# Beta and decay in v's second weight tile, retention's PSUM banks from bank 4, and unread products ahead of eight transposes

## What is computed

```python
def even_mixer(x, rel_bias, w_in, conv_w, a_log, dt_bias, norm_w, w_out):
    q_a, k_a, v_a, z_a, b_a, a_a, q_b, k_b, v_b = jnp.split(x @ w_in, EVEN_SPLITS, axis=-1)
    ...
    beta = jax.nn.sigmoid(b_a.astype(f32))
    g = -jnp.exp(a_log.astype(f32)) * jax.nn.softplus(a_a.astype(f32) + dt_bias.astype(f32))
    o_a = gated_delta_rule(q_a, k_a, v_a, g, beta)
    ...
    o_b = dilated_attention(q_b.reshape(shp), k_b.reshape(shp), v_b.reshape(shp), rel_bias)

# in diff_attention, for each head and block of 128 queries
    p = jax.nn.softmax(s, axis=-1)
    attn = p[:, :, 0] - lam * p[:, :, 1]
    return jnp.einsum('bhqk,bhkv->bhqv', attn.astype(v.dtype), vt)
```

## Time and profile before

| | us |
|---|---|
| median of 3 runs | 1760.88 |
| lowest and highest | 1760.47, 1765.22 |
| span of the profiled execution | 1759.8 |
| TensorE busy in it | 1648.0 |
| VectorE busy | 937.4 |
| ScalarE busy | 627.9 |
| GpSimd busy | 228.9 |

### The profile page before, as it was taken

The page is one execution under the profiler, slowest core; times in us unless marked ns, Lnnn a source line. Parts: engine busy times, 40 slices in busy tenths (PEclk is TensorE's granted clock), DMA queues, the critical chain, the costliest instruction groups (busy, mean ns, idle before and its releaser), DMA issues. The chain is left out here.

```text
span 1759.8 us, 25741 instructions
## 1 busy us (share of the span) xinstructions
PE 1648.0 (94%) x10372; PEld 1226.0 (70%) x10372; DVE 937.4 (53%) x1668; ACT 627.9 (36%) x1050; POOL 228.9 (13%) x217
## 2 busy tenths in 40 slices
PE   9999998999999989999999989997789999899966
PEld 8788875699988544899888864442379898643422
DVE  1285664688642565788554766131166967732212
ACT  1035322466531224566446541110144456411101
POOL 0000000054202121263101302000000300020000
PEclk9999999999999999999999999998999999999989
DMA  8322186445553666455424766999954655699996
GB/s 328 144 96 96 66 337 268 170 166 216 192 215 122 238 275 251 162 197 193 168 96 144 301 249 260 421 421 421 390 217 144 201 225 177 259 408 421 421 420 265
DMA packets 50336, 429.45 MB, mean 244 GB/s; under 512 B 5788, under 2 KB 6048, under 8 KB 9248
## 3 DMA queue, kind: packets, MB, share of 16 engines
q1 hardware_dynamic: 47232, 417.59, 61.0%
q0 software_dynamic: 2256, 7.88, 1.3%
q10 hardware_dynamic: 720, 2.23, 0.3%
HBM read 426.62 MB, written 1.05 MB: 243 GB/s over the span
## 5 line engine op out<-in xcount | busy, mean ns | idle before, releaser
L88 ACT ACTIVATE arena<-ps 128x384 f32<-128x384 f32 (+5 forms) x221 | 96.4, 436 | 512.3 <-PE ps L82 305.5
L82 PE MATMUL ps<-ringx,arena 128*64 128x512 f32 (+1 forms) x1088 | 251.0, 623 | 29.6 <-DMA ring<-in_mu 19.7
L82 PE MATMUL ps<-xsplit_f,wsplit_f 128*128 128x256 f32 x2112 | 256.0, 284 | 4.2 <-ACT xsplit_f L88 2.6
L82 PEld LDWEIGHTS ps<-xsplit_f,wsplit_f 128*128 128x128 f32 x2112 | 254.1, 192 | 6.6 <-ACT xsplit_f L88 4.2
L82 PE MATMUL ps<-ring,arena 128*64 128x512 f32 (+2 forms) x768 | 238.7, 618 | 15.7 <-DMA ringx<-in_md 6.9
L91 DVE TENSOR_TENSOR wsplit_f<-ring,wsplit_f 128x1024 fp32r<-128x1024 f32 x132 | 180.2, 1369 | 70.3 <-ACT wsplit_f L88 70.3
L82 PEld LDWEIGHTS ps<-ringx,arena 128*64 128x64 f32 (+1 forms) x1088 | 75.3, 130 | 168.7 <-issue 157.7
L82 PE MATMUL ps<-xTs,ring 128*128 128x256 f32 (+1 forms) x960 | 186.0, 353 | 2.2 <-ACT xTs L88 2.2
L82 PEld LDWEIGHTS ps<-xTs,ring 128*128 128x128 f32 x960 | 161.4, 191 | 23.3 <-issue 4.8
L88 ACT ACTIVATE wsplit_f<-ring 128x1024 fp32r<-128x1024 f32 x132 | 138.1, 1051 | 57.4 <-PE ps L82 56.5
L91 DVE TENSOR_TENSOR ringlo<-ring,ringhi 128x1024 fp32r<-128x1024 f32 x88 | 120.4, 1384 | 58.6 <-ACT ringhi L88 58.3
(11 more groups left out here) (204 smaller groups left out, 2315.8 us busy)
## 6 DMA issues: line engine op xcount, KB each, us to landing
ring<-in_wu SPq DMA_DIRECT2D x22, 2048.0 KB, 8.5
ringx<-in_mg SPq DMA_DIRECT2D x44, 1024.0 KB, 15.5
ringx<-in_mu SPq DMA_DIRECT2D x44, 1024.0 KB, 17.9
ring<-in_ada SPq DMA_DIRECT2D x20, 2048.0 KB, 8.7
ringx<-in_md SPq DMA_DIRECT2D x32, 1024.0 KB, 17.3
ring<-in_md SPq DMA_DIRECT2D x32, 1024.0 KB, 23.7
ring<-in_wd SPq DMA_DIRECT2D x10, 2048.0 KB, 8.2
ring<-in_mg SPq DMA_DIRECT2D x20, 1024.0 KB, 15.6
```

Source lines behind the costliest of these rows:

```text
L82: return self.e.matmul(o, l, r, start=start, stop=stop, skip_group_check=True)
L88: return self.e.activation(o, i, f, **k)
```

## The change

Three edits.

First, the twelve columns of beta and decay are appended to the tile wev2, which becomes 268 columns wide, and wba is gone from the parameters. wev2 is loaded and multiplied before wev. ScalarE copies the twelve columns of each half out of vb1's bank ahead of its evacuation, VectorE has no copy of its own and works out beta and decay before it evacuates vb0. The bank ba is gone, so the count of R8 is one lower in everything that follows, up to retention.

Second, warm(2) stands ahead of the wait for each of the eight softmax results in the odd mixer: 16 unread products.

Third, retention sets R8's count to 4 after its own warm(4): the first rows' transposes take banks 4 and 5, the four products 6, 7, 0 and 1, the second rows' transposes 2 and 3.

```diff
 def all_loads():
-    out = [("we", 6), ("we", 7), ("we", 8), ("wev",), ("wev2",)] + [("we", j) for j in range(6)]
+    out = [("we", 6), ("we", 7), ("we", 8), ("wev2",), ("wev",)] + [("we", j) for j in range(6)]
...
-          ("lwg", 256), ("rw", 128), ("wba", 96), ("wgd", 128)]
+          ("lwg", 256), ("rw", 128), ("wgd", 128)]
...
-        return 2048 if name[0] in ("wev2", "wdl") else 4096
+        return {"wev2": 2144, "wdl": 2048}.get(name[0], 4096)
...
+            proj_rows(("wev2",), "vb1", 268)
             proj_rows(("wev",), "vb0", 512)
-            proj_rows(("wev2",), "vb1", 256)
-            b = bank("ba")
-            wba = C("wba").rearrange("p (k n) -> p k n", k=8)
-            for h in range(2):
-                for k in range(8):
-                    r = mm(b[:, 12 * h:12 * h + 12], xT[:, k, h * 128:h * 128 + 128], wba[:, k, :], k == 0, k == 7)
-            r.then_inc(s_pe, t.did("ba"))
             t.wait_ge(s_hank, 16)
...
                 elif k == 2:
+                    warm(2)
                     t.wait_ge(*v("df_p", u))
                     b = bank("dfT", u)
...
         def ret():
             warm(4, ring=MOE_BANKS)
+            ps.turn[R8] = 4
             first_tiles(6, ("wr", 0), "pr", Q.xT)
...
-            for h in range(2):
-                evac_rows("vb0", h, E.vbt[:, h, 0:512])
-            v.note("vbt")
-            v.wait_ge(*t("ba"))
-            copy(small[:, 0:24], ps("ba")[:, 0:24]).then_inc(s_dve, v.did("free", "ba"))
-            v.note("ba")
             ba = two(small[:, 0:24])
             v.wait_ge(*a("beta_exp"))
...
                 .then_inc(s_dve, v.did("decay"))
+            for h in range(2):
+                evac_rows("vb0", h, E.vbt[:, h, 0:512])
+            v.note("vbt")
             v.wait_ge(*t("gam"))
...
             for h in range(2):
+                a.wait_ge(*t("vb1", h))
+                copy(small[:, 12 * h:12 * h + 12], ps("vb1", h)[:, 256:268]).then_inc(s_act, a.did("ba"))
                 evac_rows("vb1", h, E.vbt[:, h, 512:768])
             a.note("vbt")
             ba = small[:, 0:24].rearrange("p (t n) -> p t n", t=2)
-            a.wait_ge(*v("ba"))
```

More of the change, by code:

```diff
@@ L3502 @@
     ins["wev"] = tiles(we[:, 4620:5132], 8, 512)
-    ins["wev2"] = tiles(we[:, 5132:5388], 8, 256)
+    ins["wev2"] = tiles(_np.concatenate([we[:, 5132:5388], we[:, 3072:3084]], 1), 8, 268)
     ins["woe"] = rowtiles(a["w_out_even"][0], 4)
@@ L3544 @@
         "lwg": pad(a["gla_w_gate"][0]), "rw": tiles(a["router_w_2"], 8, 16)[0],
-        "wba": tiles(we[:, 3072:3084], 8, 12)[0], "wgd": tiles(wo[:, 3072:3088], 8, 16)[0],
+        "wgd": tiles(wo[:, 3072:3088], 8, 16)[0],
     }
```

## The result

The changed kernel takes 1746.18 us (1744.34 to 1749.63, 4 runs) against 1762.35 for the kernel before on the same chip (4 runs). The forecast was 8.5 us faster, 1752.4, with 1747.5 as the low end of the range. The sign is right, the size is little more than half of what came, and the time lies outside the range.

What follows compares the result with a forecast made beforehand. TensorE's queue was taken as the bound nearly everywhere, with DMA full in two expert stages. The terms -3.9 + 0.2 - 1.4 - 3.4 = -8.5 us gave 1752.4 us, with an 8-in-10 range of 1747.5 to 1758.5.

Steps and rivals of the forecast that it cites:

- A, the products and the wait: At v's rows: narrow products gone, second rows 12 columns wider, -3.17 us; TensorE's wait for the decay chain gone, -0.59.
- the load term: At TensorE's first weight load, about 25 us: parameter block 48 KB shorter, -0.1 us.
- Sum of A: -3.9: Beta and decay riding with v's second rows: -3.17 - 0.59 - 0.1 us, on TensorE's own queue before the attention products.
- B: Unread products ahead of the third stage's eight transposes: +1.0 us cost, one of two clock places kept, -1.4 net.
- the clock of one place: Third stage, behind the waits near 610 and 658 us: 2.4 us lost at each; the first taken as kept.
- waits as short as those at 638: Third stage: products at 638.64 ran at full speed behind waits of 0.60 and 0.58 us, so such waits do no harm.
- C: Retention's start from bank 4: TensorE starts 1.9 us earlier, plus half of the clock's gain, -3.4 us.
- the 2.9 us of clock: Retention, 1291 to 1297 us, clock 0.50: between 0 and 2.9 us kept after the shorter wait; half taken.
- What the prediction quoted from the Trainium skill on transposes: At retention's start: transposes don't count as TensorE activity, so part C keeps no clock, -1.9 us, total 1753.9.
- The shift of banks: Eight-bank ring up to retention: later tiles move one bank, one becomes later around 938 us; +0.2 us, bounds 0 and +0.5.
- The loads keep their own time: Rival: expert stages' loads not tied to earlier stages, gains become waits there; 1757.5 us or no change, chance 0.11.
- The slower rival: Third stage: unread products delay the chain they wait beside, full 6.9 us stands; +1.3, 1762.2 us, chance 0.05.

Runs made afterwards that it cites:

- e1: The changed kernel without the unread products and without retention's bank count set to 4; ratio 0.9921 to the kernel before, -13.9 us.
- e7: e1 with the eight-bank ring's count raised by one behind v's rows, so each later tile keeps its old bank; ratio 0.9933 to the kernel before.
- e11: The changed kernel with 64 unused columns behind the parameters in SBUF; ratio 0.9900 to the kernel before.
- e14: The changed kernel with unread products only before the four transposes whose waits cover them, eight in place of sixteen; ratio 0.9906 to the kernel before.
- e2: The kernel before with only the two unread products added before each of the eight softmax waits; ratio 0.9994, -1.1 us.
- e4: The changed kernel measured again as it stands; ratio 0.9907 to the kernel before, -16.4 us.

## Why the prediction was right in direction and short by nearly half

**A, the products and the wait: right, with a small term short.** -4.1 against -3.76 without the load term. The chain is hidden and nothing took its place. The 0.1 for the shorter load can't be told: at 25 us the traces lie between 0.4 us earlier and 1.2 later than the kernel before, with part A or without. The 0.4 at VectorE's copy was not in the sum.

**A, the whole: wrong, and here the prediction fell.** The step that failed is "Sum of A: -3.9", as a list of what A does. The SBUF layout wasn't in it: I costed the shorter parameter block as 48 KB less to load, and never as 384 bytes by which 81920 bytes of weight buffers move in each partition. 4.7 us came from there, and 0.8 more from the faster products at retention's end. The row that said it mattered was the earlier trace rows: two stages of 176 us with DMA share 1.00. In such a stage 1.4% on each packet is 2.5 us, and no wait has to go for it.

**The base: one profile stood for all.** In the stretch of A the profile before was faster than the five others like it, by 0.83 us or more. The measured gain is against the usual execution.

**B: right in kind.** The cost is +1.08 for +1.0 forecast. The gain is 1.6 in the mean, where the clock of one place, 2.4, was forecast: net -0.5 for -1.4. My ground for the choice, that waits as short as those at 638 do no harm, didn't hold: behind 0.77 and 0.23 the clock fell in four profiles of ten. The timed difference of B is within the interval of nothing.

**C: right in mechanism, the clock's share mis-sized.** The wait is 1.27 us, for ScalarE, as worked out. I took half of the 2.9 us of clock; in twelve profiles of twelve all of it was kept: -4.6 in the mean for -3.4. The timed -3.7 has an interval that holds both. What the prediction quoted from the Trainium skill on transposes (TensorE: Matmul & The Clock Gate, Part 4), by which the clock would be lost, didn't hold in this stretch: it was at 1.00 in the products behind eight transposes and waits of 0.64, 0.19 and 1.27 us.

**The shift of banks:** 0 for +0.2, as e1 and e7 show. **The loads keep their own time:** wrong, the gain of A and B stands behind the expert stages. **The slower rival:** wrong, as the waits of 0.77 and 0.23 show.

Put together: -4.1 - 0.4 - 0.8 - 4.7 - 0.8 - 0.5 - 4.6 = -15.9 (A's products and wait, VectorE's copy, the base, the loads, the products at retention's end, B, C), against -15.3 and -16.4 measured. The agreement is closer than the terms deserve, since several are means of profiles that differ by 1 us. Part A alone is -13.9 (-11.8 to -16.2), and its terms here add to -10.8. Another 1.6 are seen from 1283 to 1300 in the two profiles without part C, e1 and e7, where retention's first products take 7.12 and 7.16 us for 8.41. With part C they are part of its 4.6, so beside A part C adds only 3.0. What remains of A, 1.5 us, is within its interval, and its cause is open: from 285 to 300, where TensorE waits for the output weights, the ten profiles with A and without narrow products lie between a gain of 2.9 us and a loss of 0.8.

No run beats the changed kernel by more than its interval. e11 (0.9900) and e14 (0.9906) are as good, and e14 does it with half of the unread products.

## What to carry to other kernels

Removing or adding a small tensor in SBUF moves all that lies behind it. Where a stage is limited by its loads, look at where its buffers start before and after: a start on a multiple of 256 bytes was worth 1.4% of a packet's time here. A stretch of a trace that depends on the clock should be read from several executions before a term is taken from it. And unread products cost their time wherever no wait covers them, here 1.08 us in ten profiles of ten; what they gave back could not be told in the times.

## What the runs showed of the hardware

- With the DMA engines full, a packet of 8192 bytes into SBUF takes 314 ns in the mean when five of the eight buffers start 128 bytes off a multiple of 256, and 310 ns when they start on one. 64 bytes off, on the three others, cost 0.3 ns in the mean.
- 192 products of 512 columns took 229 or 234 ns from start to start, by where in SBUF their operands start (ten profiles and nine).
- 32 hardware products of 12 columns, with TensorE never idle in them, can be followed by a granted clock of 0.5: five of six profiles, and one of three with the products put back.
- Behind waits of 0.77, 0.23 and 0.58 us, 16 products ran at full speed (1.26 us) in some profiles (e2, e14) and took 2.14 and 2.22 in others (the changed kernel's, e4).
- A gap of 1.3 to 1.7 us behind eight transposes was followed by products at full speed in twelve profiles of twelve (5.60 us for 48). Behind a gap of 3.1 us they took 8.3 to 8.4 us in four profiles and 7.1 to 7.2 in two.
